# A hybrid decoder step: ring of three weight slots beside the attention heads, a fourth slot for C, the remainder of C on GpSimd, and head pieces in the middle of each chunk

## The reference

```python
s = jnp.einsum('bhik,bhjk->bhij', qc, kc) * w_intra
num = w_inter[..., None] * jnp.einsum('bhik,bhkv->bhiv', qc, C) + jnp.einsum('bhij,bhjv->bhiv', s, vc)
den = w_inter * jnp.einsum('bhik,bhk->bhi', qc, n) + jnp.sum(s, axis=-1)
h = num / jnp.maximum(jnp.abs(den), jnp.exp(-m_row))[..., None]
C_new = decay[..., None, None] * C + jnp.einsum('bhjk,bhjv->bhkv', kw, vc)
n_new = decay[..., None] * n + jnp.sum(kw, axis=2)
```

## Time and profile before

| | us |
|---|---|
| median of three runs | 2526.45 |
| the profiled execution | 2528.17 |
| its span | 2526.4 |
| TensorE busy | 2488.1 (98%) |
| VectorE busy | 1226.8 (49%) |
| ScalarE busy | 886.9 (35%) |
| GpSimd busy | 486.8 (19%) |
| attention stage, from `den` of head 0 to the last `samples_turned` | 1216.4 to 1486.2 |

### The profile page before, as it was taken

The page is one execution under the profiler, slowest core; times in us unless marked ns, Lnnn a source line. Parts: engine busy times, 40 slices in busy tenths (PEclk is TensorE's granted clock), DMA queues, the critical chain, the costliest instruction groups (busy, mean ns, idle before and its releaser), DMA issues.

```text
span 2526.4 us, 43844 instructions
## 1 busy us (share of the span) xinstructions
PE 2488.1 (98%) x16639; PEld 2439.6 (97%) x16639; DVE 1226.8 (49%) x1411; ACT 886.9 (35%) x1025; POOL 486.8 (19%) x602
## 2 busy tenths in 40 slices
PE   9999999999999999999999999999999999999998
PEld 8999999999999999999877789999999999999997
DVE  6644444444444455443677785544444344434443
ACT  5333233233333333323334453333333333333332
POOL 5430022012102232210011113221022003102221
PEclk9999999999999999999999999999999999999998
DMA  6544544454444444455455554554454445444442
GB/s 190 150 145 152 149 149 149 149 149 149 149 150 150 150 150 131 145 150 158 159 187 186 185 196 143 155 150 150 150 150 150 149 142 154 149 149 145 139 153 92
DMA packets 197127, 385.04 MB, mean 152 GB/s; under 512 B 12053, under 2 KB 12165, under 8 KB 196645
## 3 DMA queue, kind: packets, MB, share of 16 engines
q1 hardware_dynamic: 196780, 383.88, 49.7%
q0 software_dynamic: 272, 0.14, 0.0%
HBM read 361.78 MB, written 22.64 MB: 152 GB/s over the span
## 4 chain that ended last, share of the span: by engine, by line
PE 92%; DVE 4%; DMA 2%; ACT 1%; issue 0%; SPq 0%; ACTq 0%
PE G L1353 29%; PE G L1354 29%; PE G L1355 29%; DMA cst<-in_state_mlstm_C 2%; DVE c_lo L1218 1%; DVE w_lo L946 1%; PE X L1602 1%; PE X L1594 1%; PE X L1341 1%; DMA vrow<-in_mlstm_head_norm 1%; DVE cst L1286 0%; ACT c_hi L855 0%; PE X L1340 0%; PE X L1460 0%; DVE rv L1237 0%
## 5 line engine op out<-in xcount | busy, mean ns | idle before, releaser
L946 DVE TENSOR_TENSOR w_lo<-w_raw,w_hi 128x1024 fp32r<-128x1024 f32 x648 | 832.3, 1287 | 1170.5 <-ACT w_hi L699 1169.6
L699 ACT ACTIVATE w_hi<-w_raw 128x1024 fp32r<-128x1024 f32 x640 | 677.5, 1059 | 1312.5 <-PE G L1355 1305.7
L1353 PE MATMUL G<-op_hi,w_hi 128*128 128x320 f32 x2816 | 873.0, 310 | 2.2 <-DVE w_lo L946 1.5
L1354 PE MATMUL G<-op_lo,w_hi 128*128 128x320 f32 x2816 | 870.9, 309 | 0.0
L1355 PE MATMUL G<-op_hi,w_lo 128*128 128x320 f32 x2816 | 870.8, 309 | 0.0
L1353 PE MATMUL G<-a_hi,w_hi 128*128 128x320 f32 x2368 | 732.6, 309 | 0.0
L1355 PE MATMUL G<-a_hi,w_lo 128*128 128x320 f32 x2368 | 731.7, 309 | 0.0
L1354 PE MATMUL G<-a_lo,w_hi 128*128 128x320 f32 x2368 | 731.7, 309 | 0.0
L1353 PEld LDWEIGHTS G<-op_hi,w_hi 128*128 128x128 f32 x2816 | 529.6, 188 | 6.9 <-issue 2.5
L1354 PEld LDWEIGHTS G<-op_lo,w_hi 128*128 128x128 f32 x2816 | 529.5, 188 | 1.6
L1355 PEld LDWEIGHTS G<-op_hi,w_lo 128*128 128x128 f32 x2816 | 529.3, 188 | 0.0
(11 more groups left out here) (248 smaller groups left out, 989.3 us busy)
## 6 DMA issues: line engine op xcount, KB each, us to landing
w_raw<-in_ffn_w_up SPq DMA_DIRECT2D x256, 512.0 KB, 3.7
w_raw<-in_ffn_w_down SPq DMA_DIRECT2D x256, 512.0 KB, 3.8
w_raw<-in_mlstm_w_in SPq DMA_DIRECT2D x96, 512.0 KB, 3.8
cst<-in_state_mlstm_C SPq DMA_DIRECT2D x32, 512.0 KB, 4.5
out_C_sample<-cst SPq DMA_DIRECT2D x32, 512.0 KB, 3.0
w_raw<-in_mlstm_w_out SPq DMA_DIRECT2D x32, 512.0 KB, 3.9
w_raw<-in_pool_w SPq DMA_DIRECT2D x8, 512.0 KB, 10.5
xrow<-in_x_prompt SPq DMA_DIRECT2D x2, 1024.0 KB, 6.0
```

Of the source, the lines that this page charges most:

```text
L699: act.activation(w_hi[:, c % RING], w_raw[:, c % RING], ACT.Copy).then_inc(w_hi_ok, 1)
L946: v.tensor_tensor(w_lo[:, slot], w_raw[:, slot], w_hi[:, slot].bitcast(F32), ALU.subtract).then_inc(w_lo_ok, 1)
L1353: pe.matmul(G[:, m, 0:T], w_hi[:, slot, t, w], hi[:, k, :], start=first and t == 0, stop=False)
L1354: pe.matmul(G[:, m, 0:T], w_hi[:, slot, t, w], lo[:, k, :], start=False, stop=False)
```

## The change

The slot RING - 1 of `w_raw`, `w_hi` and `w_lo` is taken out of the weights' ring in the slabs S_O: these use three slots (A_RING), split two chunks ahead (A_LEAD), and go back to four at S_OUT, whose chunk 3 is loaded when all states of that slot are stored. The freed slot is the fourth slot for C, and its `w_hi` and `w_lo` a second pair of `c_hi` and `c_lo`; `qz` is doubled too. The 36 items (32 states and 4 prompt states) go round the four slots in one order; a load waits for the store of the item four before. ScalarE splits state n + 1 at the end of chunk n. `c_lo` moves from VectorE to GpSimd. On TensorE the numerator with `samples_turned`, the prompt's state, the pieces of `prep` (now at chunks 2 to 6) and `den` of the next head (chunk 7) stand in the middle of a chunk, behind two of its four banks; the sum of keys of the next head stands at the head's end. VectorE's reciprocal stands behind the last update of the head before, `num_out` after `samples_out`; `gated` is cut in two (`scaled` at chunk 4). The prompt's state moves from chunk 0 to 1. The 128x128 tile of ones becomes one column, broadcast; it makes room for the second `qz`.

```diff
+A_RING = 3
+A_LEAD = 2
...
+def o_slot(a):
+    return (a + 1) % A_RING
...
+def between(h, c):
+    if c == 0:
+        return ("num", h, 0)
+    if c == 1:
+        return ("updp", h, 0)
+    pieces = [("turn", h + 1, t) for t in range(TT)] + [("rows", h + 1, 0), ("score", h + 1, 0)]
+    return pieces[c - 2] if h + 1 < HEADS and c - 2 < len(pieces) else None
 def fill_list():
...
+ITEMS = [(h, b) for h in range(HEADS) for b in (0, "prompt", *range(1, NSEQ))]
+C_SLOTS = 4
+ITEM = {it: n for n, it in enumerate(ITEMS)}
+def c_slot(h, b):
+    return (ITEM[h, b] + 3) % C_SLOTS
...
+        c_at = [cst[:, 0], cst[:, 1], cst[:, 2], w_raw[:, RING - 1]]
+        c_hi = [c_hi1[:, :, :], w_hi[:, RING - 1]]
+        c_lo = [c_lo1[:, :, :], w_lo[:, RING - 1]]
...
             def state_load(h, b):
-                if b > 1:
-                    sp.wait_ge(c_out[c_slot(b)], 16 * (c_stores(h, b) - 1))
-                elif h:
-                    sp.wait_ge(c_out[c_slot(b)], 16 * c_stores(h - 1, b + 6))
-                sp.dma_start(cst[:, c_slot(b)], c_dram[b, h]).then_inc(c_in[c_slot(b)], 16)
+                n = ITEM[h, b]
+                if n >= C_SLOTS:
+                    sp.wait_ge(c_out[c_slot(h, b)], 16 * (c_stores(h, b) - 1))
+                elif c_slot(h, b) == C_SLOTS - 1:
+                    sp.wait_ge(w_lo_ok, chunk_no(S_QKV + 7, CH - 1) + 1)
...
+            def load_o(a):
+                h, c = a // CH, a % CH
+                if h < HEADS:
+                    sp.wait_ge(w_lo_ok, chunk_no(S_O, a) - A_RING + 1)
+                    sp.dma_start(w_raw[:, o_slot(a)], w_qkvo[c][:, :, (8 + h) * NC:(9 + h) * NC]).then_inc(w_in[o_slot(a)], 16)
+                else:
+                    sp.wait_ge(w_lo_ok, chunk_no(S_OUT, c) - A_RING + 1)
+                    sp.dma_start(w_raw[:, c], w_out[c][:, :, 0:NC]).then_inc(w_in[c], 16)
...
+            state_load(0, 1)
+            state_load(0, 2)
+            for a in range(A_RING):
+                load_o(a)
+            state_load(0, 0)
+            going = []
             for h in range(HEADS):
                 for c in range(CH):
-                    if c == 0:
-                        if h:
-                            state_load(h, 1)
+                    load_o(CH * h + c + A_RING)
+                    for it in going:
+                        if it + C_SLOTS < len(ITEMS) and ITEMS[it + C_SLOTS][1] != "prompt":
+                            state_load(*ITEMS[it + C_SLOTS])
+                    going = [ITEM[h, c]]
+                    if c == 1:
                         state_store(h, "prompt")
+                        going.append(ITEM[h, "prompt"])
                     state_store(h, c)
-                    if c + 2 < NSEQ:
-                        state_load(h, c + 2)
-                    elif c == NSEQ - 1 and h + 1 < HEADS:
-                        state_load(h + 1, 0)
-                    if h + 1 < HEADS:
-                        load(S_O + h + 1, c, w_qkvo[c][:, :, (9 + h) * NC:(10 + h) * NC])
-                    else:
-                        load(S_OUT, c, w_out[c][:, :, 0:NC])
+            for c in range(A_RING, CH):
+                if c == RING - 1:
+                    sp.wait_ge(c_out[C_SLOTS - 1], 16 * len(ITEMS) // C_SLOTS)
+                    sp.dma_start(w_raw[:, c], w_out[c][:, :, 0:NC]).then_inc(w_in[c], 16)
...
-                pool.tensor_copy(qz[:, :, :, at], q2[:, :, :, at]).then_inc(qz_ok, 1)
+                if n > 1:
+                    pool.wait_ge(qc_done, n - 1)
+                pool.memset(qz[n % 2][:, :, :, old].bitcast(F32), 0.0).then_inc(qz_ok, 1)
+                pool.tensor_copy(qz[n % 2][:, :, :, at], q2[:, :, :, at]).then_inc(qz_ok, 1)
+            def state_lo(h, b):
+                n = state_no(h, b)
+                pool.wait_ge(c_hi_ok, n + 1)
+                pool.tensor_tensor(c_lo[n % 2], c_at[c_slot(h, b)], c_hi[n % 2].bitcast(F32), ALU.subtract).then_inc(c_lo_ok, 1)
             weigh_keys(0)
             for h in range(HEADS):
-                query(h, 0)
-                if h:
-                    head_squares(h - 1)
-                for b in range(1, 4):
+                for b in range(NSEQ):
+                    state_lo(h, b)
                     query(h, b)
-                if h + 1 < HEADS:
-                    weigh_keys(h + 1)
-                for b in range(4, NSEQ):
-                    query(h, b)
+                    if h and b == 1:
+                        head_squares(h - 1)
+                    if h + 1 < HEADS and b == 4:
+                        weigh_keys(h + 1)
...
+            def split_o(a):
+                if a >= CH * HEADS:
+                    return split(S_OUT, a - CH * HEADS)
+                act.wait_ge(w_in[o_slot(a)], 16 * o_loads(a))
+                act.wait_ge(gemm, o_used(a))
+                act.activation(w_hi[:, o_slot(a)], w_raw[:, o_slot(a)], ACT.Copy).then_inc(w_hi_ok, 1)
...
+            def state_hi(n):
+                h, b = n // NSEQ, n % NSEQ
+                act.wait_ge(c_in[c_slot(h, b)], 16 * c_loads(h, b))
+                if n == 1:
+                    act.wait_ge(gemm, used(S_QKV + 7, CH - 1))
+                elif n:
+                    act.wait_ge(qc_done, n - 1)
+                act.activation(c_hi[n % 2], c_at[c_slot(h, b)], ACT.Copy).then_inc(c_hi_ok, 1)
...
+            state_hi(0)
             for h in range(HEADS):
...
-                        act.activation(cst[:, 0, 1, :], X[1][:, :], ACT.Copy).then_inc(drained_a, 1)
+                    split_o(CH * h + c + A_LEAD)
...
                         root2(h - 1)
+                    if c == 1:
+                        act.wait_ge(filled, FILL["updp", h, 0])
+                        n = ITEM[h, "prompt"]
+                        if n >= C_SLOTS:
+                            act.wait_ge(c_out[c_slot(h, "prompt")], 16 * (c_stores(h, "prompt") - 1))
+                        act.activation(c_at[c_slot(h, "prompt")][:, 1], X[1][:, :], ACT.Copy).then_inc(drained_a, 1)
+                    elif between(h, c) and c > 1:
+                        prep(h + 1, c - 2)
+                    if state_no(h, c) + 1 < NSEQ * HEADS:
+                        state_hi(state_no(h, c) + 1)
...
                 for c in range(CH):
-                    n = LEAD + c
-                    state_lo(h, c)
-                    split(S_O + h, n) if n < CH else split(S_O + h + 1, n - CH)
                     if c == 0:
...
                         if h:
-                            v.wait_ge(c_out[0], 16 * c_stores(h - 1, 5))
-                        v.tensor_copy(cst[:, 0, 0, :], X[0][:, :]).then_inc(drained, 1)
+                            samples_out(h - 1)
+                            v.wait_ge(att_s, h)
+                        link(v.tensor_copy(rds[:, :], rd[:, TP:T]))
+                        num_out(h)
+                    split_o(CH * h + c + A_LEAD)
                     if c + 1 < NSEQ:
                         key_lo(h, c + 1)
-                    if h + 1 < HEADS and 1 <= c <= TT + 2:
-                        prep(h + 1, c - 1)
+                    if c == 0:
+                        v.wait_ge(x3_filled, X3_USES[f"n{h}"])
...
+                    if c == 1:
+                        v.wait_ge(filled, FILL["updp", h, 0])
+                        n = ITEM[h, "prompt"]
+                        if n >= C_SLOTS:
+                            v.wait_ge(c_out[c_slot(h, "prompt")], 16 * (c_stores(h, "prompt") - 1))
+                        v.tensor_copy(c_at[c_slot(h, "prompt")][:, 0], X[0][:, :]).then_inc(drained, 1)
+                    elif between(h, c) and c > 1:
+                        prep(h + 1, c - 2)
                     if h and c == 3:
                         mean_square(h - 1)
+                    if h and c == 4:
+                        scaled(h - 1)
                     if h and c == 5:
                         gated(h - 1)
...
                     if c == CH - 1:
+                        if h + 1 < HEADS:
+                            den_kept(h + 1)
...
-                        st = cst[:, c_slot(c), t, :]
+                        st = c_at[c_slot(h, c)][:, t]
...
+                if h + 1 < HEADS:
+                    link(v.reciprocal(rd[:, :], rd[:, :]))
...
+            def halfway(h, c):
+                if c == 0:
+                    if h:
+                        samples_turned(h - 1)
+                    num(h)
+                elif c == 1:
+                    prompt_state(h)
+                elif between(h, c):
+                    prep(h + 1, c - 2)
+                elif c == CH - 1 and h + 1 < HEADS:
+                    den(h + 1)
+            den(0)
+            keys_sum(0)
+            for h in range(HEADS):
...
                 for c in range(CH):
-                    s = S_O + h
...
+                    chunk(o_slot(CH * h + c), op_hi, op_lo, CK * c, c == 0, c == CH - 1, free, None, lambda: halfway(h, c))
+                    if h and c == 2:
+                        head_norm_sum(h - 1)
```

(8 more changed lines are left out.)

240 lines of the change are left out of this document (129 added, 111 removed).

## The result

The changed kernel takes 2514.19 us (median of four runs, 2511.87 to 2519.78). The kernel before, on the same chip, takes 2527.92. The ratio is 0.9946, with a 95% interval of 0.9931 to 0.9961. That is 13.7 us less, where the forecast was 21 less (2505.5, off the median of 2526.45 that was known then). The same kernel on another chip gave 0.9947 (0.9929 to 0.9964).

A forecast was written before the change was run, and what follows sets the result against it. TensorE, 98% busy, was taken as the bound, with 26.0 us of stalls and half clock to win in heads 1 to 3; -26.0 + 2 + 1 + 1 + 1 = -21 off the median 2526.45 gave 2505.5 us, range 2497 to 2516.

The forecast's parts named there:

- What bounds the kernel: Attention stage, heads 1 to 3: stalls around loads and splits of C, and half clock, make 26.0 us of excess.
- the yardstick: Head 0 of the attention stage, 61.5 us and nearly free of stalls, from which the other heads' stall-free lengths were derived.
- The lateness by the lock: GpSimd's c_lo and VectorE exclude each other, so w_lo comes late: 2 us over four heads, bounds 0 and 5.
- The fourth slot: Loads of C start three chunks earlier: at least 5 us of room instead of 1.3, ending the 14.4 us of waits.
- The second pair: Second c_hi/c_lo lets ScalarE split state n+1 while TensorE is at state n; worth a chunk of 5.4 us.
- rival 1: The hand-off of C through GpSimd stays tight: half of 24 chunks lose 0.8 us, 9.6 more, 2515; chance 0.18.
- Pieces in the middle, den and keys_sum: TensorE's head pieces moved within chunks and den, keys_sum to the head's end: cost 1 us, between -1 and +2.6.
- Ring of three: Three weight slots for o, split two chunks ahead: cost 1 us, up to 4 if landings stretch in head 3.
- The end of the stage: w_out's weights for slot 3 load only after the last C is stored: cost 1 us, bounds 0 and 3.
- The sign of being wrong: The forecast is wrong if the first slab of w_out shows a gap over 3 us or heads exceed 67.
- Rival 2: VectorE, not the slot, was the bound in the stage: gain only about 9 us, 2517.5; chance 0.09.
- Rival 3: Every VectorE instruction excludes GpSimd's, so heads last as long as both together: slower, 2541; chance 0.04.

The follow-up runs named there:

- the second execution: The changed kernel profiled and timed once more, on another chip, with no edit: 2515.63 us, 0.9947 of the kernel before.
- f4: The changed kernel with the edits of f1, f2 and f3 together: 2503.66 us, 0.9898 of the kernel before.
- f2: The changed kernel with key_lo of chunk 1 ahead of num_out, and head 0's sum of keys in the middle of its first chunk: 2513.26 us, 0.9924.
- e4: The changed kernel with its four slots kept, but each load of C issued one chunk later: 2534.33 us, 1.0019 of the kernel before.
- e3: The changed kernel with only one pair of c_hi and c_lo in use at a time: 2520.19 us, 0.9953 of the kernel before.
- e2: The changed kernel with the head pieces behind the whole chunk instead of in its middle: 2519.34 us, 0.9953 of the kernel before.
- f1: The changed kernel with the weights of the o slabs issued one chunk earlier: 2511.86 us, 0.9925 of the kernel before.
- f3: The changed kernel with chunks 3 and 4 of w_out loaded from within head 3: 2513.66 us, 0.9936 of the kernel before.
- after: The changed kernel itself, in its first profiled execution and its timed runs: 2514.19 us, 0.9946 of the kernel before.

## Why the prediction was right or wrong

**Direction and range: right.** Faster by 13.7, in the range of 2497 to 2516, 8.7 us above the forecast.

**What bounds the kernel: right.** The stage had 26 us to give, in waits for C and the half clock behind them. Heads 1 and 2 came to 63.6 and 63.5, where 63 to 66 stood; head 3 to 57.6, where 57 to 60 stood; the clock was 1.00 (0.97 in head 2 of the second execution); of TensorE's wait for `c_lo` at most 0.6 was left; ScalarE's waits for C fell from 76.6 to 3.7. That the floor can be reached is shown by f4: its 243.7 is what the yardstick gave (269.8 - 26.0 = 243.8).

**The lateness by the lock, 2 of bounds 0 to 5: mechanism right, place and size wrong.** In 27 of its 32 instances `c_lo` takes 2.34 to 2.47 on GpSimd, in the other five 2.6 to 3.2 (estimate 2.41). I looked for its price at `w_lo`, which has two chunks of cover, and in head 3. It showed at a short instruction without cover: `key_lo` at the start of heads 1 to 3, blocked by `head_squares` (2.59 instead of 0.48). I costed the lock by instruction and not by position: "up to 2.4 in each chunk" was written down for the one instruction that could bear it. f2 took 3.6 back by moving `key_lo`.

**The fourth slot: the lead right, one sum wrong.** e4 shows that the gain is gone without the lead of the loads, and its trace leaves 4.2 to 6.2 us of room at the state that was followed, where "at least 5" stood. For the kernel before, the hand-off was added up wrongly: 1.4 + 0.4 + 4.55 + 1.06 + 1.23 is 8.6 and not 8.2, so its room was 0.9 and not 1.3, which only strengthens the argument.

**The second pair "worth a chunk of 5.4 us": wrong,** nothing shows of it (e3). It wasn't in the sum, but it was my argument against rival 1. That rival's repeated waits for `c_lo` didn't come either. In e3, where the pair is out of use, they hold 1.0 us, and in e4, where the lead is, 14.2: the lead covers them and not the pair.

**Pieces in the middle, den and keys_sum, 1 of -1 to +2.6: right.** The sum started from all 26, so this term was the price over a stage without stalls. Of it the runs show the sum of keys of head 0, which stood right behind `den` and waited 1.2 us for VectorE's reciprocal; f2 took that back. For the switches between formats nothing was left to pay: f4 has all 26 pieces in the middle and reaches the floor. What the place itself brings, 3 to 5 us against pieces behind the chunk (e2), was put down to the slots. I had described why, with X0 and X1 wanted by the update of C and by the piece one after the other, and given it no number.

**Ring of three, 1 of 0 to 4: not contradicted.** f1's stage is 1.8 shorter, which two executions of one kernel can differ by. ScalarE's 44.0 us of waiting were nearly all idle time.

**The end of the stage, 1 of 0 to 3: mis-sized.** 3.0 and 3.6 in the two executions; f3 took the 3.0 away. The price of the weights alone was right: `w_lo` of chunk 3 was there 11.2 us behind the stage's end, where 10.5 to 12 stood, and TensorE took it up without a wait. The step that failed is the one behind it, written down as "the later third chunk eats into it". The loads of two more chunks stood behind that one, VectorE makes all three `w_lo` ahead of `a_lo`, and TensorE waits 2.5 us for `a_lo` of head 3, the longest single wait of the table. The sign of being wrong that was written down, a gap over 3 us in that slab, was just missed.

**The sum.** The forecast was a stage of 247.8, 4 over the floor, and 1 more behind it. After's stage is 6.8 over the floor: 3.6 for `key_lo`, 1.2 for the sum of keys, and up to 1.8 for the weights. Behind it are 3.0. That is 4.8 short of the forecast; in the second execution the lost race adds 2.5 and the part behind 0.6, together 7.9, where 21 were forecast and 13.0 came. No term stood for the lost race.

**Rivals.** Rival 1 (2515) names the number best and the wrong cause: behind GpSimd's hand-off TensorE waited 0.6 us and not 9.6. That it came nearest is luck. Rival 2 (2517.5), that VectorE becomes the bound, names the cause: all but 1.5 us of the waits that were left are VectorE's, but they come to 8 us and not to what it priced. VectorE's busy share in the stage, 196 of 251, is not the reason; the order at four places is. Rival 3, that the lock takes all, is refuted by the time and by the updates of C: they read PSUM and SBUF, and take 740 ns on the average, 739 before. Of it remains that 29 of the 39 us moved off VectorE came back as blocking. The Trainium skill, page "SBUF — State Buffer", section "Who interferes with whom", says that two SBUF inputs make the difference; the trace agrees at 484 against 2660 ns for the key products. The warning of the Trainium skill, page "Perfetto Trace Analysis", section "Optimizing Scalar/DVE Operations", that such a move might not help, is right for after (0 to 2.5 us) and not for f4 (5 to 6).

## What to carry to other kernels

Cost an exclusion between two engines by where the short instructions stand that nothing covers, not by the mean length of those with cover: here a half-microsecond product grew to 2.6 at the start of three heads and was mended by putting it two steps earlier. Moving work between the two engines also moves the instant at which the blocking falls, so look again for what stands there. Where an engine works in program order, ask of each moved load what stands behind its split: the weights came in time, and the remainder queued behind them held a whole slab. A claim of room can be tested by issuing the load one step later, if one checks that the load still lands as fast; and a second profile of the same kernel says how much of a difference of 2 us is the kernel's.

## What the runs showed of the hardware

A VectorE instruction of two SBUF inputs on only 64 partitions is held for the whole of a GpSimd instruction too: 2.59 instead of 0.48, begun 0.01 us behind one of 2.32. The price over a stage in which VectorE is busy for four fifths was 0.9 us for each GpSimd instruction of 2.4.

A stretch of 17.1 us at half clock that begins 24 us into the program (20.5 us from 21.6 in f2) came in some executions, of kernels whose code there is the same, and not in others; in after it put the stage 7.8 us later. The profile of before doesn't have it, but its times have the same gap (2536.46 to 2539.24 in three runs of one chip, 2527.34 to 2530.92 in the eight others); that it is the same stretch isn't shown. In after it begins amid the mixer's small fp32 products, with no idle time of TensorE just before it; the second execution of after ran them at full clock. What sets it off stays open.

A load of 512 KB issued within 0.1 us behind another one landed in 6.1 us (median of 22 in e4), where one issued 2 us or more behind it landed in 4.0 (after).
